# Splitting the gate's product in the RWKV stage, with pair 1 in plain float32 while the parts are made

## What is computed

```python
h = jnp.concatenate([x, dx], axis=-1) @ w_comb       # x plus a share of dx, each output kind with its own share
r, k, v, g, w_lo, a_lo = jnp.split(h, list(np.cumsum(widths)[:-1]), axis=-1)
w = -jax.nn.softplus(-(w0 + jnp.tanh(w_lo) @ w2)) - 0.5
a = jax.nn.sigmoid(a0 + a_lo @ a2)
kk = (k * k_k); kk = kk / jnp.maximum(jnp.linalg.norm(kk, axis=-1, keepdims=True), 1e-12)
k = k * (1 + (a - 1) * k_a)
decay = jnp.exp(-jnp.exp(w.astype(jnp.float32)))
```

## Time and profile before

| | |
|---|---|
| median of three runs | 2305.42 us |
| the profiled execution, its own time | 2304.1 us |
| its span, first to last instruction | 2302.3 us |
| TensorE busy | 2135.9 us (93%) |
| VectorE, ScalarE, GpSimd busy | 54%, 38%, 41% |
| mean granted TensorE clock | 0.972 |
| stage A | 0 to 515 us |
| DMA | 198 MB, mean 86 GB/s |

### The profile page before, as it was taken

How to read it: one execution, slowest core, us unless ns; L and a number is a source line. 1 busy time by engine, 2 the same in 40 slices (tenths; PEclk the granted TensorE clock), 3 DMA queues, 4 the chain that set the end, 5 groups by cost and what they waited for, 6 DMA issues and landing times.

```text
span 2302.3 us, 57462 instructions
## 1 busy us (share of the span) xinstructions
PE 2135.9 (93%) x23316; PEld 1802.0 (78%) x23316; DVE 1236.8 (54%) x1982; ACT 876.0 (38%) x2220; POOL 949.0 (41%) x609
## 2 busy tenths in 40 slices
PE   6799999989999999997989999999899899998997
PEld 4698888978888888886989966777699676776775
DVE  8665566654566666655125614444510576428674
ACT  1744444434555555554332122333323201302351
POOL 1133343323323322335535821222434498456355
PEclk8899999999999999997999999999999999999999
DMA  2234434455433443433222220100112322221102
GB/s 95 94 147 154 149 147 150 153 156 142 80 76 68 95 86 63 90 69 118 89 74 74 92 73 28 37 24 30 37 56 96 109 91 64 73 74 64 46 1 73
DMA packets 158986, 198.00 MB, mean 86 GB/s; under 512 B 121040, under 2 KB 123344, under 8 KB 156496
## 3 DMA queue, kind: packets, MB, share of 16 engines
q1 hardware_dynamic: 158800, 195.25, 28.2%
HBM read 156.24 MB, written 38.99 MB: 85 GB/s over the span
## 4 chain that ended last, share of the span: by engine, by line
PE 59%; issue 6%; DVE 4%; POOL 4%; ACT 2%; POOLq 1%; DVEq 0%; DMA 0%; ACTq 0%; SPq 0%
PE wide L849 9%; PE wide L1336 9%; PE wide L1337 9%; PE wide L1338 9%; PE wide L1979 5%; PE wide L2098 3%; PE wide L1867 2%; PE wide L2052 1%; PE wide L2691 1%; PE wide L2082 1%; PE wide L2371 1%; PE wide L2674 1%; POOL x_w L1146 1%; PE wide L874 1%; PE wide L2056 1%
## 5 line engine op out<-in xcount | busy, mean ns | idle before, releaser
L1336 PE MATMUL wide<-mixed_high,w_high_rwkv_in 128*128 128x264 f32 x720 | 211.0, 293 | 12.0 <-ACT k L457 7.3
L1338 PE MATMUL wide<-mixed_high,w_low_rwkv_in 128*128 128x264 f32 x720 | 206.1, 286 | 0.0
L1146 POOL TENSOR_TENSOR x_w<-n,masks 128x192 f32<-128x192 f32 x48 | 28.8, 600 | 360.8 <-ACT n L1019 360.8
L580 POOL TENSOR_TENSOR w_low_rwkv_in<-weights,w_high_rwkv_in 128x1024 fp32r<-128x1024 f32 x45 | 107.7, 2407 | 162.4 <-ACT w_high_rwkv_in L446 162.4
L362 PE MATMUL wide<-mixed_in,weights 128*128 128x264 f32 x672 | 161.6, 399 | 12.4 <-DVE mixed_in L332 12.3
L362 PEld LDWEIGHTS wide<-mixed_in,weights 128*128 128x128 f32 x672 | 128.4, 194 | 45.6 <-issue 16.5
L1336 PEld LDWEIGHTS wide<-mixed_high,w_high_rwkv_in 128*128 128x128 f32 x720 | 137.4, 191 | 25.7 <-issue 15.2
L1357 POOL TENSOR_TENSOR w_high<-weights,con 128x1024 fp32r<-128x1024 f32 x45 | 108.8, 2417 | 74.1 <-PE wide L1338 46.8
L1338 PEld LDWEIGHTS wide<-mixed_high,w_low_rwkv_in 128*128 128x128 f32 x720 | 137.5, 191 | 0.0
L849 PE MATMUL wide<-x_w,n_levels 64*64 64x64 f32 x2752 | 121.1, 223 | 6.0 <-DVE x_w L1098 1.6
L849 PE MATMUL wide<-e,x_w 64*64 64x64 f32 x2752 | 121.4, 220 | 0.5 <-ACT e L1031 0.2
(11 more groups left out here) (403 smaller groups left out, 6404.3 us busy)
## 6 DMA issues: line engine op xcount, KB each, us to landing
weights<-in_stream SPq DMA_DIRECT2D x200, 512.0 KB, 3.5
forms<-form SPq DMA_DIRECT2D x16, 2020.5 KB, 6.3
forms_in<-forms SPq DMA_DIRECT2D x96, 144.0 KB, 4.4
forms_in<-forms SPq DMA_DIRECT2D x32, 288.0 KB, 4.5
gate_bonus<-forms SPq DMA_DIRECT2D x16, 576.0 KB, 4.0
r_ahat_r<-forms SPq DMA_DIRECT2D x32, 144.0 KB, 3.6
mixed<-gate_bonus SPq DMA_DIRECT2D x14, 264.0 KB, 2.1
gated<-mixed SPq DMA_DIRECT2D x14, 264.0 KB, 4.7
```

The costliest lines, as they stand in the source:

```text
L580: pool.tensor_tensor(w_in[1][:, at, :], ring.slot(load), w_in[0][:, at, :].bitcast(F32), ALU.subtract).then_inc(w_split, 1)
L1336: pe.matmul(dst, w[0], x[0], start=start, stop=False)
L1338: return pe.matmul(dst, w[1], x[0], start=False, stop=stop)
```

## The change

- g is split too, from pair 3 on. Its input gets a low part, `low_g`, so there are 32 input tiles to split rather than 24.
- Pair 1 is plain float32 in all four products; k, r and v are split from pair 2 on (`SPLIT_FROM = (2, 2, 2, 3)`).
- The input parts are made inside pairs 0 to 2: pieces of the work (`act_in_low`, `act_in_high`, `dve_in_low`) are placed between the steps of ScalarE and VectorE.
- The two slots of the weight parts now serve k and v, and r and g. ScalarE rounds k's weights of the next pair where it did; r's weights of the next pair only after tanh of g and the small copy; g's weights right after the copy of r, ahead of the two tanh.
- Temporary rows share memory: the running sum is made over the decay, 1/P over the running sum (with a wait between the two exponentials), the new k over k, tanh of g over k (with waits for GpSimd's first product and for VectorE's step 7), the root over the square, and the halved bias replaces the parameters themselves.

```diff
-        a_r, a_k, a_lw, a_cum, a_a, a_kk, a_sq, a_inv, a_k2, a_rk, a_tg, a_Pinv = (
-            sa(n, LP) for n in ("r", "k", "log_decay", "log_cum", "a", "kk", "kk_sq", "kk_inv", "k2", "rk", "tanh_g", "p_inv"))
+        a_r, a_k, a_lw, a_a, a_kk, a_sq, a_rk = (sa(n, LP) for n in ("r", "k_or_tanh_g", "decay", "a", "kk", "kk_sq_or_inv", "rk"))
+        a_tg, a_inv = a_k, a_sq
...
+        SPLIT_FROM = (2, 2, 2, 3)
+        WHOLE_FROM = max(SPLIT_FROM)
...
         def act_weights(act, i, j):
 
-            before, step = ((3, i - 1), (2, i - 1), (1, i))[j]
             ring.wait_full(act, 1 + j, i)
-            ring.wait_used(act, before, step)
-            act.activation(w_in[0][:, (1 + j) % 2, :], ring.slot(1 + j), ACT.Copy).then_inc(w_high, 1)
+            if not isinstance(i, int) or i >= WHOLE_FROM:
+                before, step = ((3, i - 1), (4, i - 1), (1, i), (2, i))[j]
+                ring.wait_used(act, before, step)
+            elif j == 2:
+                ring.wait_used(act, 1, i)
+            act.activation(w_in[0][:, slot_in(i, j), :], ring.slot(1 + j), ACT.Copy).then_inc(w_high, 1)
...
             act.activation(real(a_r), wide[3][:, :, 0:HALF], ACT.Copy).then_inc(s["r_copied"], 1)
+            if 3 in split_in(i):
+                act_weights(act, i, 3)
...
-            act.activation(a_P[:, :, 1:], by_chunk(a_cum[:]), ACT.Exp).then_inc(EXP_A.sem, 1)
-            act.activation(a_Pinv[:], a_cum[:], ACT.Exp, scale=-1.0).then_inc(EXP_A.sem, 1)
+            act.activation(a_P[:, :, 1:], by_chunk(a_lw[:]), ACT.Exp).then_inc(EXP_A.sem, 1)
+            act.wait_ge(EXP_A.sem, EXP_A.at(i, 1))
+            act.activation(a_lw[:, PAD:], a_lw[:, PAD:], ACT.Exp, scale=-1.0).then_inc(EXP_A.sem, 1)
+            if turned:
+                turned()
...
-            if first:
-                act.wait_ge(s["lerp"], 6 * KD)
-            if not last:
+            to_come = [] if last else split_in(i + 1)
+            if 0 in to_come:
                 act_weights(act, i + 1, 0)
-                act_weights(act, i + 1, 1)
+            if ended:
+                ended()
             ring.wait_used(act, 4, i)
+            act.wait_ge(POOL_A.sem, POOL_A.at(i, 1))
+            act.wait_ge(DVE_A.sem, DVE_A.at(i, 7))
             act.activation(real(a_tg), wide[1][:, :, 0:HALF], ACT.Tanh, scale=0.5).then_inc(s["g_tanh"], 1)
             act.wait_ge(EXP_A.sem, EXP_A.at(i, 1))
             act.activation(f_pc, a_P[:, :, C:C + 1].rearrange("p c n -> p (c n)"), ACT.Copy).then_inc(s["pc_copied"], 1)
+            if 1 in to_come:
+                act_weights(act, i + 1, 1)
...
+        def act_a(act):
+            act_pair(act, 0, True)
+            act_in_low(act, IN_K)
+            act_in_low(act, IN_R[:4])
+            act_pair(act, 1, False, squared=lambda: (act_in_low(act, IN_R[4:]), act_in_high(act, IN_K)),
+                     turned=lambda: act_in_low(act, IN_V), ended=lambda: act_in_high(act, IN_R[:4]))
+            act_pair(act, 2, False, begin=lambda: (act_in_high(act, IN_R[4:]), act_in_high(act, IN_V)),
+                     squared=lambda: act_in_low(act, IN_G))
+            act_in_high(act, IN_G)
+            with act.Fori(WHOLE_FROM, PAIRS - 1) as i:
+                act_pair(act, i, False)
+            act_pair(act, PAIRS - 1, False, last=True)
...
-        def dve_pair(dve, i, first):
+        def dve_pair(dve, i, first, rests=(), late_rests=()):
...
             step(dve.tensor_scalar(a_kk[:], a_k[:], rw(KK, i), None, ALU.mult))
+            dve_in_low(dve, rests)
...
-            step(dve.scalar_tensor_tensor(a_rk[:], a_r[:], rw(RK, i), a_k2[:], ALU.mult, ALU.mult))
+            step(dve.scalar_tensor_tensor(a_rk[:], a_r[:], rw(RK, i), a_k[:], ALU.mult, ALU.mult))
+            dve_in_low(dve, late_rests)
...
-                for j in range(SPLIT):
-                    load, at = 1 + j, (1 + j) % 2
-                    pool.wait_ge(w_high, SPLIT * i + (j + 1 - SPLIT))
+                for j in split_in(i):
+                    load, at = 1 + j, slot_in(i, j)
+                    pool.wait_ge(w_high, splits_at(i, j))
                     pool.tensor_tensor(w_in[1][:, at, :], ring.slot(load), w_in[0][:, at, :].bitcast(F32), ALU.subtract).then_inc(w_split, 1)
...
+        def dve_a(dve):
+            dve_pair(dve, 0, True)
+            dve_in_low(dve, IN_K)
+            dve_pair(dve, 1, False, rests=IN_R, late_rests=IN_V)
+            dve_pair(dve, 2, False, late_rests=IN_G)
+            with dve.Fori(WHOLE_FROM, PAIRS) as i:
+                dve_pair(dve, i, False)
```

## The result

The changed kernel takes 2315.21 us (median of four runs, 2313.7 to 2316.89), the kernel before 2304.96 us beside it (2300.54 to 2305.7). The ratio is 1.0049, 95% interval 1.0036 to 1.0061: slower by 0.5%, some 10 us, where 2292 was forecast. The profiled execution took 2313.98 us with a span of 2312.1 us, 9.8 more than before. In three of them (the short rest of g, the rests behind pair 2, the table ahead) the median counts one slow execution (3412, 8263 and 5141 us), which moves it by 0.8 us at most, and the ratio leaves it out.

A forecast was written before the change was run, and what follows sets the result against it. TensorE's own list of matmuls was taken to bound the loop. Profiled 2304.1 - 16.3 (g split) + 3 (pairs 1 to 3) = 2290.8 us; the median stands 1.3 above, so 2292, range 2285 to 2313.

The forecast's parts named there:

- the shorter g: TensorE's loop pairs: split g takes 5.96 us instead of 7.32, saving 1.36 us a pair, 16.3 us in 12 pairs.
- The rest of k: Loop: GpSimd's low weights of k done 6.68 us behind the start of ScalarE's copy of v, 0.3 ahead of k; no cost.
- The table load: Loop, ScalarE: tanh's table is loaded behind the wait for g, taking 1.28 us, not while g still runs.
- VectorE's undisturbed 15 steps: Loop: they end 12.16 us behind the start of ScalarE's copy of v, 0.8 us ahead of r.
- The step that failed: Loop: VectorE asks for step 13 9.49 us behind v's copy start, GpSimd for r's rest at 9.65; VectorE goes first.
- g's rest might hold L527: Loop: GpSimd's low weights of g may hold VectorE's short step, scan and exponentials 1.8 to 2.1 us later; cost taken as 0.
- rival 1: Loop: GpSimd asks before VectorE's step 13, which waits a whole operation; pairs 0.1 to 0.4 us slower, 2313 us; chance 0.27.
- The start: Pairs 1 to 3: ScalarE's copy of v in pair 3 starts at 175.5 us, 3 us later than before; bounds -2 to +7.
- The three waits: Pairs 2 and 3: TensorE idles 3.5 us ahead of r, 3 ahead of v, 8.4 ahead of pair 3's r.
- The slow clock: Start: TensorE at half speed for about 3 us after idling, 1.6 us lost, once or twice.
- Rivals 2 and 3: Loop: 2, low weights of r or k late, 2297 us, chance 0.12; 3, split g no shorter, 2308 us, chance 0.03.
- the drain of 1.38 us: ScalarE's table loads: left out; with it r would wait some 0.5 us a pair, taking 6 us of the gain.

The follow-up runs named there:

- the short rest of g: Changed kernel with GpSimd making only 128 of 1024 columns of g's low weights, the others left from an earlier product: 2289.43 us, ratio 0.9919 to the kernel before.
- the rests behind pair 2: Changed kernel with VectorE's 8 rests of g's input tiles behind pair 2, not between its steps 7 and 8: 2305.32 us, ratio 1.001 to the kernel before.
- the table ahead: Changed kernel with ScalarE's small copy ahead of the tanh of g and only the wait for g right before that tanh: 2311.59 us, ratio 1.0028.
- the doses above: Changed kernel with ScalarE rounding r's weights in 1, 2, 4 or 8 instructions: 2315.21, 2321.87, 2290.4 and 2284.16 us.
- the runs with pieces: Changed kernel with ScalarE rounding r's weights in four or eight instructions instead of one: 2290.4 and 2284.16 us.
- the run with two pieces: Changed kernel with ScalarE rounding r's weights in two instructions instead of one: 2321.87 us, ratio 1.0069 to the kernel before.
- eight pieces: Changed kernel with ScalarE rounding r's weights in eight instructions instead of one: 2284.16 us, ratio 0.9915 to the kernel before.

## Why the prediction was wrong

**What held.** The bound and the method: the shorter g uncovered VectorE's chain, as the prediction feared. TensorE's list per pair is 26.27 us where nothing waits, 1.26 less than before (1.36 forecast). The rest of k is done at 346.39 + 2.42 = V + 6.74 (6.68). The table load stands behind the wait for g, GpSimd asks for r's rest at V + 9.67 (9.65), and VectorE's undisturbed 15 steps fit in front of r.

**The step that failed.** "VectorE asks for L561 (step 13, two inputs from SBUF) at V + 512.60 - 503.11 = V + 9.49", and with it "VectorE goes first". It asks at V + 9.78. The V + 9.49 came from the last pair, with the remark that GpSimd is idle there. It is so only from 504.71 us (V + 1.60) on, when its second product for `form` is over; and a loop pair of the kernel before has step 8 (L545) free just the same, since GpSimd's products end at V + 1.62:

```profile
310.27 1.80 POOL L587 TENSOR_TENSOR form<-r,p_cum 128x576 f32<-128x576 f32 x1
...
313.64 0.43 DVE L545 TENSOR_SCALAR kk_inv<-kk_inv 128x528 f32<-128x528 f32 x1 [2.71 <-ACT kk_inv L478]
```

So no pair of the kernel before showed the hold; it comes with the change, which moves those products against V. The prediction did see that g's rest might hold L527, priced that by what it does to the exponentials and V, and set it "between 0 and 0.1 us a pair". For V that is right: the exponentials end at 342.00, just ahead of the copy at 342.07:

```profile
341.35 0.65 ACT L493 ACTIVATE decay<-decay 128x528 f32<-128x528 f32 x1
342.07 0.61 ACT L499 ACTIVATE form<-wide 128x528 f32<-128x528 f32 x1
342.75 1.28 ACT L503 ACT_TABLE_LOAD   x1
344.04 1.19 ACT L503 ACTIVATE kk_sq_or_inv<-wide 128x264 f32<-128x264 f32 x3
```

But steps 4 to 6 stand behind the same scan in VectorE's list, and GpSimd's two products wait for step 6, which was not followed: they run until V + 3.62 instead of V + 1.87 (in the run with the short rest of g, 330.69 + 1.82), and step 8, asked at V + 3.19, is held 0.29 us. Those 0.29 us against a margin of 0.16 turned the order. Of the consequences of a held step one was followed and the other not.

The Trainium skill ("SBUF — State Buffer", Who interferes with whom) lists `tensor_scalar`, which has one tensor as its source, among the operations that can take a two-port mode and then contend with GpSimd. The prediction cited it and kept it inside its bound for want of a row; the 2.17 against 0.43 us of step 2 and the 0.72 against 0.43 of step 8 agree with that list. The same section of the Trainium skill says that the issue order decides who blocks; the doses above agree: with GpSimd first by 0.02 us VectorE's step 13 takes 2.96 us, and with VectorE first by 0.15 us it takes 0.71 and GpSimd's operation 2.85.

**Sizes inside rival 1.** The mechanism and place of the rival were right, VectorE's end at V + 14.63 too (14.5 or 14.6). It put r "up to 0.39 us later" than V + 14.31; r starts at 356.94, V + 14.87, 0.56 later, since 0.24 us pass between the end of step 15 and the first matmul. The pair is 0.67 longer; the last 0.11 fall between the start of r and the next V (13.34 us, 13.23 before). Twelve times 0.67 is 8.1 and not 4.7. The rival's 0.27 was too low beside 0.58 for a decision within 0.16 us that hangs on a sum of terms from different pairs.

**The start.** "V of pair 3 is 175.5, 3 us later than before": it is 172.84, no later. The three waits are where they were put, each shorter: 2.2, 1.8 and 7.7 us (3.5, 3 and 8.4). The three in TensorE's timeline:

```profile
118.16 0.59 PE L1381 MATMUL wide<-mixed_high,w_high_rwkv_in 128*128 128x264 f32 x1 [2.20 <-DVE form L609]
...
128.68 0.36 PE L1381 MATMUL wide<-mixed_high,w_high_rwkv_in 128*128 128x264 f32 x1 [1.82 <-issue]
...
157.06 0.56 PE L1381 MATMUL wide<-mixed_high,w_high_rwkv_in 128*128 128x264 f32 x1 [7.74 <-DVE form L609]
```

VectorE ends pair 1 at 118.1 instead of 121: V of pair 1 is 102.94 and not 104.5, and the steps behind it take 15.16 us and not 16.5. In pair 2 it starts on step 8 at 148.05 and not 151.6. The slow clock came twice, as the estimate allowed: behind the first wait (0.54 and 0.61 from 118 to 122 us) and behind the third (0.50 from the start of r at 157 to 162 us, longer than the 3 us assumed), and not behind the second. One microsecond at the start is in no term of the change: V of pair 0 is 69.98 in this execution and 70.96 in that of before. That it has the other sign than the loop's error was luck: the start hid 3 us of it.

**Rivals 2 and 3.** The low weights of r are there at V + 12.10 (351.74 + 2.43), ahead of the V + 13.1 at which TensorE could use them, and at V + 12.8 in the runs with pieces, where TensorE does not wait either; the split g is shorter and its own weights are there. Both are out. The same holds for the drain of 1.38 us that the Trainium skill ("ScalarE: Activation LUTs", What ACT_TABLE_LOAD costs) adds to each load. None is to be seen here: the tanh follows right behind its load (rows below), and the load for the root stands 0.07 us behind the end of the copy of v, with the root right behind it (342.75 and 344.04 above).

```profile
348.70 1.28 ACT L513 ACT_TABLE_LOAD   x1 [2.39 <-PE wide L1383]
350.00 0.61 ACT L513 ACTIVATE k_or_tanh_g<-wide 128x528 f32<-128x528 f32 x1
```

## What to carry to other kernels

Where two engines exclude each other, don't ask only how long each operation takes but who asks first, and by how much; if the margin is smaller than what any hold upstream can add, treat the order as open, give it half the chance, and follow every consumer of a step that may be held, not only the one on the path. Such a meeting is cheap to repair: delaying the engine with slack (four small roundings instead of one, +0.3 us) was worth some 25 us here, while making its data ready 1.5 us sooner was worth 0.05 us a pair. And a chain's length measured before the change holds only while its neighbours stand where they stood: where a change moves one of them against the chain, as GpSimd's products moved here from V + 1.62 to V + 3.62, lay the moved operation over every step of the chain.

## What the runs showed of the hardware

- A one-source step of VectorE in SBUF (128x528, 0.43 us) is held by GpSimd like a two-source one: 2.17 us behind a rest that began 0.55 us earlier, and a step with only 2 columns takes 0.45 us behind GpSimd's product, against 0.17 where nothing holds it (pair 0 of the same run).
- A request of VectorE's 0.02 us behind GpSimd's (by the recorded starts) pays the whole operation, 2.96 us for 0.71; one 0.15 us ahead pays nothing, and GpSimd's operation is stretched by the 0.4 us instead. A queue of VectorE steps back to back does not keep GpSimd out: in the changed kernel it asks at 351.74, VectorE's step 12 ends at 351.81 and step 13 is issued at 351.85, too late.
- TensorE's clock stayed at 1.00 over eleven pairs with a wait of up to 1.7 us in each. In the run with two pieces it fell to 0.50, the lower of its two levels (1.2 GHz), behind a wait of 1.78 us (336 to 338 us), in seven of twelve pairs and not in the other five; that cost 1.5 us more in such a pair. In the changed kernel's start it fell behind waits of 2.20 and 7.74 us and not behind one of 1.82 us. What decides, no run here shows.
- The clock in the first 40 us differs between executions of nearly the same program: from 20 to 40 us it is 0.54 in the profiled execution of the kernel before and 1.00 in that of the changed one. V of pair 0 does not follow it: it is 71.65 and 71.58 at 1.00 (the rests behind pair 2, eight pieces) and 70.21 at 0.57 (the table ahead), so what moves the start by up to 1.8 us stays open.
